# A fused two-block model: copies behind later tiles, a weight unit rounded beside the norm, the last two pairs of the feed-forwards in another order

## What is computed

```python
# block 1, after the mixers
h = h + rmsnorm(mix, attn_post_norm)
u = rmsnorm(h, ffn_pre_norm)
gate, up = jnp.split(u @ w_gate_up, [D_FF], axis=-1)      # D_FF = 2816
y = (jax.nn.silu(gate) * up) @ w_down
h = h + rmsnorm(y, ffn_post_norm)
h = h + (p @ ple_proj) * jax.nn.sigmoid(h @ ple_gate)
...
# block 2, after the mixers
x = x + conv_ffn(rms_norm(x, ffn_norm_g), w_gate, w_up, conv_w, conv_b, w_down)   # causal conv of width 3 on the gate
gate = jax.nn.sigmoid(rms_norm(x, ple_norm_g) @ w_ple_gate)
x = x + gate * (p_2 @ w_ple_proj)
```

## Time and profile before

| | |
|---|---|
| median of 3 runs | 3175.54 us (3169.97 to 3178.27) |
| the profiled execution | 3176.49 us, its span 3174.9 us |
| mean granted clock of TensorE | 0.964 |
| busy: PE, DVE, ACT, POOL | 94%, 50%, 32%, 4% |
| rounding a unit: `w_hi`, `w_lo` | 1.05 us, 1.25 us (means of 215) |
| a square on ScalarE, start to start in a row | 0.95 us |
| landing: weight unit, p | 3.6 us, 5.8 us (medians, whole span) |

### The profile page before, as it was taken

One profiled execution on the slowest core, in us unless ns is written; L12 is line 12 of the kernel. 1 busy time (PEld: TensorE's weight loads), 2 busy tenths in 40 slices (PEclk: granted clock), 3 DMA queues, 4 the chain that ended last, 5 costly groups with the idle time before them and its releaser, 6 DMA issues.

```text
span 3174.9 us, 35161 instructions
## 1 busy us (share of the span) xinstructions
PE 2996.1 (94%) x14780; PEld 2498.6 (79%) x14780; DVE 1572.5 (50%) x1986; ACT 1018.1 (32%) x1377; POOL 117.2 (4%) x66
## 2 busy tenths in 40 slices
PE   8999989997999999999999977899999999999998
PEld 6888878886788888887778856788878888888877
DVE  4256766524443443345642277577435454445454
ACT  3143445433211111112431166676322211212131
POOL 0011211022000000000100000000000000000000
PEclk9999989998999999999999978998999999999999
DMA  4101220032111111111121100000211111111122
GB/s 159 54 27 54 82 86 1 27 101 92 60 47 49 52 40 53 54 47 40 47 86 60 34 14 9 21 1 1 100 34 53 47 47 54 47 54 47 49 77 80
DMA packets 45805, 165.59 MB, mean 52 GB/s; under 512 B 5424, under 2 KB 5936, under 8 KB 45648
## 3 DMA queue, kind: packets, MB, share of 16 engines
q1 hardware_dynamic: 45648, 163.34, 15.7%
HBM read 142.09 MB, written 21.23 MB: 51 GB/s over the span
## 4 chain that ended last, share of the span: by engine, by line
PE 87%; DVE 7%; ACT 3%; issue 2%; DMA 0%; SPq 0%; ACTq 0%; DVEq 0%
PE PS L274 22%; PE PS L276 22%; PE PS L278 22%; PE PS L476 2%; PE PS L477 2%; PE PS L478 2%; PE PS L1184 2%; PE PS L699 2%; PE PS L2654 1%; PE PS L1154 1%; PE PS L1169 1%; PE PS L2208 1%; PE PS L2176 1%; DVE w_lo L268 1%; PE PS L2645 1%
## 5 line engine op out<-in xcount | busy, mean ns | idle before, releaser
L274 PE MATMUL PS<-u_hi_f,w_hi 128*128 128x512 f32 x1408 | 440.9, 395 | 27.2 <-DVE u_lo_f L395 15.1
L276 PE MATMUL PS<-u_lo_f,w_hi 128*128 128x512 f32 x1408 | 437.6, 392 | 0.0
L278 PE MATMUL PS<-u_hi_f,w_lo 128*128 128x512 f32 x1408 | 437.5, 392 | 0.0
L268 DVE TENSOR_TENSOR w_lo<-w_raw,w_hi 128x1024 fp32r<-128x1024 f32 x215 | 267.8, 1254 | 290.9 <-ACT w_hi L262 290.9
L262 ACT ACTIVATE w_hi<-w_raw 128x1024 fp32r<-128x1024 f32 x215 | 225.6, 1052 | 572.5 <-PE PS L278 431.8
L274 PEld LDWEIGHTS PS<-u_hi_f,w_hi 128*128 128x128 f32 x1408 | 266.7, 190 | 87.2 <-DVE w_lo L268 13.9
L276 PEld LDWEIGHTS PS<-u_lo_f,w_hi 128*128 128x128 f32 x1408 | 267.4, 190 | 56.4
L278 PEld LDWEIGHTS PS<-u_hi_f,w_lo 128*128 128x128 f32 x1408 | 266.8, 190 | 56.0
L274 PE MATMUL PS<-f_ah,w_hi 128*128 128x512 f32 x704 | 218.5, 392 | 10.3 <-DVE f_al L1687 10.3
L276 PE MATMUL PS<-f_al,w_hi 128*128 128x512 f32 x704 | 218.1, 391 | 0.0
L278 PE MATMUL PS<-f_ah,w_lo 128*128 128x512 f32 x704 | 217.9, 391 | 0.0
(11 more groups left out here) (381 smaller groups left out, 4980.1 us busy)
## 6 DMA issues: line engine op xcount, KB each, us to landing
w_raw<-in_weights SPq DMA_DIRECT2D x217, 512.0 KB, 3.6
H<-in_x_t SPq DMA_DIRECT2D x16, 512.0 KB, 4.4
stick_kept<-stick_stage SPq DMA_DIRECT2D x12, 512.0 KB, 2.9
mixer<-stick_kept SPq DMA_DIRECT2D x9, 512.0 KB, 6.9
p_kept<-p_stage SPq DMA_DIRECT2D x8, 512.0 KB, 4.0
h_kept<-H SPq DMA_DIRECT2D x8, 512.0 KB, 5.7
H<-h_kept SPq DMA_DIRECT2D x8, 512.0 KB, 7.2
p_pp<-p_kept SPq DMA_DIRECT2D x8, 512.0 KB, 6.4
```

What stands on the lines that cost most here:

```text
L268: dve.tensor_tensor(self.w_lo[i][:], self.w_raw[i][:], self.w_hi[i][:].bitcast(F32), ALU.subtract).then_inc(*self.s("w_lo").up(g))
L274: ins = e.matmul(banks[i], lh, rh[i], start=first, stop=False)
L276: ins = e.matmul(banks[i], lh, rl[i], start=False, stop=False)
L278: ins = e.matmul(banks[i], ll, rh[i], start=False, stop=last)
```

## The change

- ScalarE's copies of the embeddings' products 5, 6 and 7 move: 5 behind the high part of k = 3, 6 behind k = 5, 7 behind the second square. TensorE's order there is the same.
- The fourth unit (`gates[0] + RING`, `base + RING`) is rounded in the norm and no longer in the loop of tile 0: in the first feed-forward ahead of root and inversion on both engines, in the second and in the second embedding stage between root and rows on ScalarE and behind the diagonal on VectorE.
- In both feed-forwards the units are laid out so that gate and up of tiles 20 and 21 are followed by the down pairs 9 and 10. Tiles 20 and 21 get buffers of their own (`ah_last`, `al_last`); the last pair begins with its first unit on chunks 0 and 1 and then the second unit on both. The splits of the last units move with it.
- The two loads of `p` (n = 0) move from early in the tile loop to behind the last up product, into other slots, and a wait of SyncE for stores goes with them.

```diff
@@ memory @@
-        self.p_raw = [[tile(f"p{n + 1}_raw{k}", (49, 44)[n] + k)[:] for k in range(2)] for n in range(2)]
+        self.p_raw = [[tile(f"p{n + 1}_raw{k}", (34, 44)[n] + k)[:] for k in range(2)] for n in range(2)]
@@ ff_units @@
-        for i in range(FF_TILES // 2 - 1):
+        for i in range(FF_TILES // 2 - 2):
             at = base + 4 + 6 * i
             gates[2 * i + 2], downs[i], ups[2 * i + 2] = at, at + 1, at + 3
             gates[2 * i + 3], ups[2 * i + 3] = at + 4, at + 5
-        downs[FF_TILES // 2 - 1] = base + 4 + 6 * (FF_TILES // 2 - 1)
+        at = base + 4 + 6 * (FF_TILES // 2 - 2)
+        for j in range(2):
+            gates[FF_TILES - 2 + j], ups[FF_TILES - 2 + j] = at + 2 * j, at + 2 * j + 1
+            downs[FF_TILES // 2 - 2 + j] = at + 4 + 2 * j
         return gates, ups, downs
+    def ff_parts(self, n, t):
+        if t < FF_TILES - 2:
+            return self.ah[n][:, t % 2, :], self.al[n][:, t % 2, :]
+        return self.ah_last[n][t % 2][:], self.al_last[n][t % 2][:]
@@ pe_down @@
+        last = i == FF_TILES // 2 - 1
+        order = [(c, k) for c in range(KT) for k in range(2)]
+        if last:
+            order[0:4] = [(0, 0), (1, 0), (0, 1), (1, 1)]
+        for c, k in order:
+            p, w, cc = self.ff_down_pair(i, c), (g + k) % RING, self.chunk(c)
+            ah, al = self.ff_parts(n, 2 * i + k)
+            if k == 0:
+                self.claim(p, dve=1)
+            if c == 0:
+                pe.wait_ge(*self.s("w_lo").at(g + k))
+            mm = self.mm3(self.halves(p), self.w_hi[w][:, cc], self.w_lo[w][:, cc],
+                          [ah[:, h * HALF:(h + 1) * HALF] for h in range(2)],
+                          [al[:, h * HALF:(h + 1) * HALF] for h in range(2)], k == 0, k == 1)
+            if c == KT - 1:
+                mm.then_inc(*self.s("w_used").up(g + k))
+            elif k:
@@ act_ffn1_head @@
-            if k in (1, 3, 5):
-                self.act_p2_step(5 + k // 2)
+            if k in (3, 5):
+                self.act_p2_step(5 + k // 4)
         self.act_split(U_FF1 + 2)
-        self.act_squares("f1", [self.f_gate[0][:], self.f_prod[0][:]])
+        for k in range(KT):
+            self.act_square("f1", k, [self.f_gate[0][:], self.f_prod[0][:]])
+            if k == 1:
+                self.act_p2_step(7)
@@ pe_ffn @@
-            if t >= 2 and t % 2 == 0:
+            if t % 2 == 0 and t < FF_TILES - 2:
                 self.pe_down(n, t // 2 - 1, downs[t // 2 - 1])
             self.pe_product(ups[t], pu, U)
+        for i in range(FF_TILES // 2 - 2, FF_TILES // 2):
+            self.pe_down(n, i, downs[i])
         self.claim(3)
-        self.pe_down(n, FF_TILES // 2 - 1, downs[FF_TILES // 2 - 1])
@@ act_ffn, ahead of the tiles @@
-        self.act_statistics(tag, self.f_rows[n][:])
+        if n == 0:
+            self.act_split(gates[0] + RING)
+        self.act_statistics_root(tag)
+        if n:
+            self.act_split(gates[0] + RING)
+        self.act_statistics_rows(tag, self.f_rows[n][:])
@@ act_ffn, in the tiles @@
-            self.act_split(gates[t] + RING)
-            if t >= 2 and t % 2 == 0:
+            if t:
+                self.act_split(gates[t] + RING)
+            if t >= 2 and t % 2 == 0 and t < FF_TILES - 2:
                 for j in range(2):
                     self.act_split(downs[t // 2 - 1] + j + RING)
             act.wait_ge(*self.s("f_gated").at(n, t))
-            if t >= 2:
+            if 2 <= t < FF_TILES - 2:
                 act.wait_ge(*self.s("w_used").at(downs[t // 2 - 1] + 1))
-            act.activation(self.ah[n][:, t % 2, :], prod[:], ACT.Copy).then_inc(*self.s("f_ah").up(n, t))
+            act.activation(self.ff_parts(n, t)[0], prod[:], ACT.Copy).then_inc(*self.s("f_ah").up(n, t))
@@ act_ffn, behind the tiles @@
+            self.act_split(downs[i - 1] + j + RING)
+        if n == 0:
@@ dve_down, in the chunks @@
+            if i == FF_TILES // 2 - 2 and c == KT - 1:
+                self.dve_split(g + RING)
@@ dve_ffn, ahead of statistics (n = 0) and behind them (n = 1) @@
+            self.dve_split(gates[0] + RING)
@@ dve_ffn, behind the tiles @@
+        self.dve_down(n, i - 1, downs[i - 1])
+        self.dve_split(downs[i - 1] + 1 + RING)
@@ sp_ffn @@
-            if n == 0 and g == base + 2 * RING:
-                for i in range(5, KT):
-                    sp.wait_ge(*self.d(f"p2_stored{i % 3}").at(i))
+            if n == 0 and g == base + 67:
+                sp.wait_ge(*self.s("w_used").at(self.ff_units(0)[1][FF_TILES - 1]))
@@ act_ple2 @@
-        self.act_statistics("p2", self.p_rows[:])
+        self.act_statistics_root("p2")
+        self.act_split(base + RING)
+        self.act_statistics_rows("p2", self.p_rows[:])
@@ dve_ple2 @@
+        self.dve_split(base + RING)
```

More of the change, by code:

```diff
@@ L168, in memory @@
         self.al = [tile(f"f{n}_al", 44, 2, F32R) for n in (1, 2)]
+        self.ah_last, self.al_last = ([[tile(f"f{n + 1}_{part}_last{j}", slots[n][j], dt=F32R) for j in range(2)]
+                                       for n in range(2)]
+                                      for part, slots in (("ah", ((49, 26), (33, 17))), ("al", ((50, 27), (41, 18)))))
         self.f_gate = [tile(f"f{n}_gate", 46) for n in (1, 2)]
@@ L1671, in dve_ffn @@
                 dve.tensor_tensor(sg[:], self.pair(pg), rows[:], ALU.mult).then_inc(*self.dve_frees(pg, tag, "gate", t))
-            self.dve_split(gates[t] + RING)
-            if t >= 2 and t % 2 == 0:
+            if t:
+                self.dve_split(gates[t] + RING)
+            if t >= 2 and t % 2 == 0 and t < FF_TILES - 2:
                 i = t // 2 - 1
@@ L1686, in dve_ffn @@
                     dve.wait_ge(*self.d(f"p2_stored{i % 3}").at(i))
-            dve.tensor_tensor(self.al[n][:, t % 2, :], prod[:], self.ah[n][:, t % 2, :].bitcast(F32),
-                              ALU.subtract).then_inc(*self.s("f_al").up(n, t))
+            ah, al = self.ff_parts(n, t)
+            dve.tensor_tensor(al, prod[:], ah.bitcast(F32), ALU.subtract).then_inc(*self.s("f_al").up(n, t))
             self.dve_split(ups[t] + RING)
         i = FF_TILES // 2 - 1
+        self.dve_down(n, i - 1, downs[i - 1])
+        self.dve_split(downs[i - 1] + 1 + RING)
         if n == 0:
@@ L1807, in act_ple2 @@
             act.activation(t, t, ACT.Sigmoid).then_inc(*self.s("p_gate").up(1, j))
-            self.act_split(base + j + RING)
+            if j:
+                self.act_split(base + j + RING)
     def dve_ple1(self):
@@ L1841, in dve_ple2 @@
             self.dve_gate(1, j, t, self.pp[1][j])
-            self.dve_split(base + j + RING)
+            if j:
+                self.dve_split(base + j + RING)
     def dve_gate(self, n, j, t, embedded):
@@ L2890, in ffn @@
         for g in range(n):
-            if g:
-                u += chan(gate, 2 * g * P)
+            u += chan(gate, 2 * g * P)
+            if 0 < g < n - 1:
                 u += rows(down, 2 * g - 2) + rows(down, 2 * g - 1)
-            else:
-                u += chan(gate, 0)
             u += chan(up, 2 * g * P) + chan(gate, (2 * g + 1) * P) + chan(up, (2 * g + 1) * P)
-        return u + rows(down, 2 * n - 2) + rows(down, 2 * n - 1)
+        for k in range(2 * n - 4, 2 * n):
+            u += rows(down, k)
+        return u
     w1 = np.asarray(inp["w_in"])[0]
```

## The result

The changed kernel takes 3125.57 us (median of 4 runs, 3124.37 to 3127.17) against 3175.68 in the same comparison; the ratio is 0.9845, 95% interval 0.9833 to 0.9857. The forecast was 3127 us, 3119 to 3142. The medians differ by 50.1 us. In the comparison of experiments 1 to 4 one of nine executions of the kernel before took 11683 us, and their ratios are without it.

The account below looks back on a forecast made before the run. The chain that ended last is 87% TensorE, so only its waits and half-clock running move the end. Six savings sum to 48.8 us: 3176.5 - 48.8 = 3127.7, 3127 us against the median, range 3119 to 3142.

Parts of the forecast that it names:

- six terms: Savings at six places where TensorE waits: 16.1 + 7.5 + 6.9 + 7.2 + 7.7 + 3.4 = 48.8 us.
- 7.5 + 6.9: First feed-forward: 7.5 us saved at its fourth weight unit, 6.9 us at its last down pair.
- 7.2 + 7.7: Second feed-forward: 7.2 us saved at its fourth unit, 7.7 us at its last down pair.
- The head's chain: First feed-forward's head: VectorE keeps ahead of TensorE, low part 3 by 1.9 us, part 5 by 2.1.
- the 2.7 us of the upper bound: Head: TensorE's wait if GpSimd's zeroing of Y delays the add and low part 5; nothing was charged.
- the rival of the head's own chain: Head stays paced by its own chain, two of three waits stay whole, 10.7 us come back: 3138; chance 0.15.
- The new wait: First feed-forward's norm: TensorE waits 1.2 us for ScalarE's copy of the norm's rows.
- the 3 us of the upper bound: First feed-forward's norm: 3 us come back if the clock falls behind the wait for the rows; not charged.
- The low part of tile 1: Second feed-forward's start: ends at 2393.2, the first down pair asks at 2393.6, so 0.4 us in time.
- The second unit: Last down pair: its second unit is ready 0.95 us after the pair before ends, asked for at 2.72.
- that term: Second embedding stage's fourth unit: rounding it earlier saves 3.4 us.
- The slower rival: Denser matmuls lose clock in the feed-forwards' tiles; a 3% loss would give 3217 us; chance 0.02.

Follow-up runs that it names:

- experiment 1: Kernel before with only the moved copies of the embeddings' products: 3156.62 us, ratio 0.9941.
- experiment 2: Kernel before with only the fourth unit's earlier rounding, in all three stages: 3153.24 us, ratio 0.9940.
- experiment 3: Kernel before with only the last two pairs of both feed-forwards in the new order: 3158.12 us, ratio 0.9947.
- experiment 4: Changed kernel with the last pair's chunks in the plain order (first unit, second unit, chunk by chunk): 3126.10 us.
- experiment 7: Changed kernel with the adds to H exchanged in both heads (VectorE even k, GpSimd odd k): 3115.70 us, ratio 0.9815 to the kernel before.
- experiment 5: Changed kernel with the copy of product 5 alone put back behind k = 1: 3131.10 us.
- experiment 11: Changed kernel with the adds to H exchanged in the first feed-forward's head alone: 3118.18 us, ratio 0.9818.

## Why the prediction was right

**The sum.** Each of its six terms was a window's length less its matmuls at full speed, and each was paid back: head 16.1 forecast, 15.9 measured; first feed-forward 7.5 + 6.9 = 14.4, measured 14.4; second 7.2 + 7.7 = 14.9, measured 15.0; second embedding stage 3.4, measured 3.3. Experiments 1 to 3 show the parts by themselves: 15.8, then 7.3, 7.1 and 3.4, then 7.0 and 7.7. The window of the head begins with the last matmul before the wait, so 97 matmuls at 0.2267 us lie in it and not 96, and it gives 15.9, which is what was measured. Counting the idle time alone would have given 3 x 3.5 + 4.5 + 5.3 + 5.6 + 5.1 + 3.1 = 34 us: the other 15 us were half clock behind the waits, and TensorE's busy time fell by 17.1. That the median came out 1.4 us under the forecast is within what untouched code moves by itself; so much of the hit is luck.

**The head's chain.** The forecast's margins came from a like chain in another stage: 1.9 us for part 3 and 2.1 for part 5. Measured they are 1.9 and 1.7. Step 2 starts at 752.95, right behind product 5, and with 2.72 us for each step or product step 3 starts at 755.67 and step 5 at 763.83; part 3 ends at 753.75 and part 5 at 762.16. (The forecast's own step times are one matmul, 0.2 us, too early, for the reason told above; by the right ones it would have had 2.1 and 2.3.)

```profile
752.50 0.62 PE L282 MATMUL PS<-p_in_hi,w_lo 128*128 128x512 f32 x2
752.95 0.62 PE L278 MATMUL PS<-u_hi_f,w_hi 128*128 128x512 f32 x2
```

```profile
747.89 3.40 DVE L438 SCALAR_TENSOR_TENSOR Y<-Y,gains,Y_rows 128x1024 f32<-128x1024 f32 x1
...
752.47 1.28 DVE L399 SCALAR_TENSOR_TENSOR u_lo_f<-H,gains,u_hi_f 128x1024 fp32r<-128x1024 f32 x1
...
755.25 3.26 DVE L399 SCALAR_TENSOR_TENSOR u_lo_f<-H,gains,u_hi_f 128x1024 fp32r<-128x1024 f32 x1 [0.30 <-ACT u_hi_f L394]
...
759.74 1.22 DVE L448 TENSOR_TENSOR H<-H,Y 128x1024 f32<-128x1024 f32 x1
760.88 1.28 DVE L399 SCALAR_TENSOR_TENSOR u_lo_f<-H,gains,u_hi_f 128x1024 fp32r<-128x1024 f32 x1
```

```profile
746.86 3.35 POOL L455 TENSOR_TENSOR H<-H,Y 128x1024 f32<-128x1024 f32 x1 [6.01 <-DVE Y L438]
755.03 2.40 POOL L455 TENSOR_TENSOR H<-H,Y 128x1024 f32<-128x1024 f32 x1 [4.82 <-DVE Y L438]
757.48 7.24 POOL L1746 MEMSET Y<- 128x1024 f32 x8
```

The head has four blocks, as many as the chain that the forecast copied, but not on adds alone, of which the forecast had spoken. Beside the first add (3.30 us) and a rounding of a unit (3.38) a scaling (3.40) and low part 4 (3.26) were blocked. The last two are fused operations with two SBUF inputs (SBUF is the on-chip memory that holds the tiles), and both ended 1.08 us after GpSimd's add. The zeroing of Y, 7.24 us in a row of eight, blocked nothing: the add at 759.74 and low part 5 inside it took 1.22 and 1.28. So the 2.7 us of the upper bound did not come, and the rival of the head's own chain did not come about, with 1.7 us left where it was closest. The Trainium skill ("SBUF — State Buffer", Who interferes with whom) says that a VectorE instruction with two SBUF inputs contends with a GpSimd instruction that reads SBUF and not with one that only writes it. These rows agree: 3.26 us beside the add, 1.22 and 1.28 beside the zeroing.

**The norm.** Copy 7 ends at 773.40, 1.3 us before TensorE's third product at 774.71 (forecast 1.3). The new wait is the one forecast:

```profile
772.39 1.01 ACT L1501 ACTIVATE p_stage<-PS 128x1024 f32<-128x1024 f32 x1
```

```profile
791.11 0.71 PE L278 MATMUL PS<-u_hi_f,w_hi 128*128 128x512 f32 x2 [1.21 <-ACT f_rows L346]
```

Its 1.21 us against 1.2; the clock stayed up (0.71 for the row, then 0.62), so the 3 us of the upper bound did not come.

**The second feed-forward's start.** The low part of tile 1 was to be 0.4 us in time. It ends at 2359.56, and TensorE's down pair starts at 2359.85, 0.3 us later. It is the closest of the forecast's margins, and it held:

```profile
2358.33 1.23 DVE L1724 TENSOR_TENSOR f_al<-f_prod,f_ah 128x1024 fp32r<-128x1024 f32 x1 [1.13 <-ACT f_ah L1610]
```

```profile
2359.85 0.62 PE L278 MATMUL PS<-f_ah,w_hi 128*128 128x512 f32 x2
```

**The last pairs.** The second unit was forecast ready 0.95 us behind the pair before and came at 1.23; asked for at 2.72. Experiment 4 shows that even this was more than enough.

**What was loose.** From one execution the forecast read that an idle time of 3.06 us leaves the clock up. Experiments 1 and 3 have the same idle time (3.05) with the clock down behind it, so that term could have been 3.4 or some 5 to 6 us (78.8 and 79.9 against 73.8 to 73.9 where the wait is gone). That the trace read from had the lower value, and its repeat too, was luck. The slower rival has no support: 650 us of the changed kernel's tiles (800 to 1450 us, above) are as busy and at the same clock 1.00 as in the earlier trace rows.

## What to carry to other kernels

Price a wait of TensorE as a window from the last matmul before it to where the matmuls run at full pace again, less the matmuls at full pace: a third of the gain here was clock, not idle time. Take the price from more than one execution where the wait is about 3 to 3.5 us, since the clock behind such a wait was up in some traces here and down in others, 3 us apart. Waits whose causes are removed in stages in series added up here to within 0.5 us; check for each what comes next and how late it is. When two traces differ, compare the stretches between marks, and then what the clock did behind each wait. Short waits behind a long one may cost more than their length: with two of 0.62 and 0.72 us gone the head fell by 4.2 us.

## What the runs showed of the hardware

- The same idle time of 3.05 to 3.06 us before the fourth unit of the second embedding stage was followed by full clock in two traces and by half clock in two, at once or three rows later (the stretch that holds it took 77.2 us twice, 78.8 and 79.9). An idle time of 3.47 to 3.53 us before one step of the first embedding stage was followed by full clock in three traces (experiments 2, 3 and 7) and by half clock, at once or three rows later, in four (both of the kernel before, experiments 5 and 11).
- Code that no edit touched took 690.8 to 691.9 us in four traces and 694.8 to 695.1 in nine (second mixers, from the sums of their input's norm to those of the second feed-forward's). The two groups part 175 to 225 us behind those sums: there the granted clock was 0.57 and then 0.84 in the changed kernel (two windows of 25 us), and 0.70 and 1.00 in experiment 7. In the kernel with the adds exchanged in the first head, one execution of five was 5.8 us and more over the rest, and its trace is one of the nine. What decides it was not found. So differences of 4 us between whole runs are no proof of a change's worth here; the stretches between marks are better evidence.
- GpSimd's add of 128 x 1024 took 2.40 us where it stood before VectorE's operations and 3.35 where one of those with two SBUF inputs was under way.
